# Expert loop of a hybrid decoder layer: next rows transposed before the gate/up products, the activation's transposes amid them, two result buffers, one load per weight matrix

## The reference, cut to what matters

```python
g = jnp.einsum('td,edf->tef', tb, w_eg)
u = jnp.einsum('td,edf->tef', tb, w_eu)
act = jax.nn.silu(g) * u * gb[:, :, None].astype(tb.dtype)
return jnp.einsum('tef,efd->td', act, w_ed)      # + shared expert, times the adaLN gate, plus x
```

## Time and profile before

| | us |
|---|---|
| median of 3 runs | 2066.68 (2063.21 to 2070.07) |
| the profiled execution | 2074.8 |
| its span, first to last instruction | 2072.8 |
| TensorE busy | 1651.7 (80%) |
| VectorE busy | 1330.2 (64%) |
| ScalarE busy | 926.2 (45%) |
| mean DMA rate | 174 GB/s; 335 to 352 GB/s in most of the expert stage |

### The profile page before, as it was taken

The page is one execution under the profiler, slowest core; times in us unless marked ns, Lnnn a source line. Parts: engine busy times, 40 slices in busy tenths (PEclk is TensorE's granted clock), DMA queues, the critical chain, the costliest instruction groups (busy, mean ns, idle before and its releaser), DMA issues.

```text
span 2072.8 us, 23077 instructions
## 1 busy us (share of the span) xinstructions
PE 1651.7 (80%) x7242; PEld 1276.1 (62%) x7243; DVE 1330.2 (64%) x1717; ACT 926.2 (45%) x1132; POOL 314.2 (15%) x282
## 2 busy tenths in 40 slices
PE   6697797799698798796975737899999669999860
PEld 1484685687476485584764625777777557777750
DVE  2486476546637657666446556788888337887859
ACT  2226425423233232322332225677777347777740
POOL 1000000000200202002100071123233122223210
PEclk9698998899699798897898867999999789999985
DMA  8110220244033050240520138899999449999948
GB/s 267 67 62 21 69 74 21 102 134 151 0 122 101 21 179 24 61 163 0 189 73 20 41 115 293 296 349 342 345 352 372 159 183 330 334 335 335 326 180 365
DMA packets 126064, 361.42 MB, mean 174 GB/s; under 512 B 21164, under 2 KB 31600, under 8 KB 115344
## 3 DMA queue, kind: packets, MB, share of 16 engines
q1 hardware_dynamic: 98352, 295.20, 41.0%
q0 software_dynamic: 22688, 45.29, 5.9%
q10 hardware_dynamic: 4928, 19.78, 2.4%
HBM read 352.18 MB, written 43.66 MB: 191 GB/s over the span
## 4 chain that ended last, share of the span: by engine, by line
PE 51%; DMA 24%; DVE 11%; ACT 6%; issue 5%; POOL 2%; POOLq 1%; ACTq 0%; SPq 0%; DVEq 0%
DMA y_rows<-yb,row_of 21%; PE psum L1188 13%; PE psum L1189 13%; PE psum L1190 13%; ACT yb L756 3%; PE psum L1388 2%; POOL slot_table L493 2%; PE psum L1210 1%; DVE ofin L864 1%; PE psum L1368 1%; PE psum L1342 1%; PE psum L1314 1%; DMA ysum<-y_rows 1%; PE psum L1399 1%; DMA rawm<-in_w_exp_down 1%
## 5 line engine op out<-in xcount | busy, mean ns | idle before, releaser
L784 DVE TENSOR_TENSOR ring<-rawm,ring 128x2048 fp32r<-128x2048 f32 x192 | 433.8, 2287 | 85.9 <-ACT ring L715 85.9
L715 ACT ACTIVATE ring<-rawm 128x2048 fp32r<-128x2048 f32 x192 | 355.4, 1908 | 31.1 <-DMA g_dram<-g2b 15.9
L1188 PE MATMUL psum<-ring,xT 128*128 128x512 f32 x528 | 219.5, 416 | 49.6 <-DVE xT L792 49.1
L1485 DVE TENSOR_TENSOR hl<-raw,hl 128x2048 fp32r<-128x2048 f32 x59 | 134.4, 2291 | 143.8 <-ACT hl L996 143.3
L1189 PE MATMUL psum<-ring,xT 128*128 128x512 f32 x528 | 211.9, 401 | 0.0
L1190 PE MATMUL psum<-ring,xT 128*128 128x512 f32 x528 | 211.5, 401 | 0.3 <-issue 0.3
L1188 PE MATMUL psum<-hl,hT 128*128 128x512 f32 x416 | 165.1, 397 | 11.2 <-DVE hT L1762 11.2
L996 ACT ACTIVATE hl<-raw 128x2048 fp32r<-128x2048 f32 x59 | 112.0, 1910 | 129.0 <-PE psum L1190 93.6
L1189 PE MATMUL psum<-hl,hT 128*128 128x512 f32 x416 | 162.9, 392 | 0.0
L1190 PE MATMUL psum<-hl,hT 128*128 128x512 f32 x416 | 162.8, 391 | 0.0
L1188 PEld LDWEIGHTS psum<-ring,xT 128*128 128x128 f32 x528 | 102.9, 195 | 84.3 <-DVE xT L792 41.1
(11 more groups left out here) (370 smaller groups left out, 3092.0 us busy)
## 6 DMA issues: line engine op xcount, KB each, us to landing
rawm<-in_w_exp_gate SPq DMA_DIRECT2D x128, 512.0 KB, 7.9
rawm<-in_w_exp_up SPq DMA_DIRECT2D x128, 512.0 KB, 10.7
rawm<-in_w_exp_down SPq DMA_DIRECT2D x64, 1024.0 KB, 6.8
raw<-in_w_in SPq DMA_DIRECT2D x36, 1024.0 KB, 5.2
raw<-in_w_ada SPq DMA_DIRECT2D x24, 1024.0 KB, 5.2
ysum<-y_rows ACTq DMA_DIRECT2D x16, 1024.0 KB, 9.0
raw<-in_w_branch_b SPq DMA_DIRECT2D x8, 1024.0 KB, 5.3
raw<-in_w_branch_a SPq DMA_DIRECT2D x4, 1024.0 KB, 5.1
```

Of the source, the lines that this page charges most:

```text
L715: A(ring[:, slot, 1, :], rawm[slot][:], ACT.Copy).then_inc(S["m_hi2"], 1)
L784: TT(ring[:, slot, 0, :], rawm[slot][:], ring[:, slot, 1, :].bitcast(F32), ALU.subtract).then_inc(S["m_lo2"], 1)
L1188: M(dst, lhs(0), rhs(0), start=first, stop=False)
L1485: TT(h_[:, 1, :], r, h_[:, 0, :].bitcast(F32), ALU.subtract).then_inc(S["lo_done"], 1)
```

## The change

Six edits, all in the expert stage.

- On TensorE the 8 transposes of the next rows come ahead of the 24 gate/up matmuls, and the 2 transposes of the activation of expert e-1 come after 12 of the 24. ScalarE and VectorE get the matching order: x_hi and x_lo first; ScalarE's three splits are spread over the iteration.
- yb has two buffers, each with its own semaphore (m_y0, m_y1). Place for it comes from `act`, which now lies over `upper`, a constant of the dense part.
- Each weight matrix is one load of 1 MB (8 KB in one run for each partition), three for an expert and not five; the gate/up slots wait for `xt_ps`.
- The hardware loop has 10 passes of six iterations in place of 20 of three, so that the parity of yb is known in the code.
- GpSimd issues the gather of the first extra rows one expert ahead (`first_more_rows`).
- Two pairs of semaphores of the dense part (dtT and lgT) become one pair (not shown).

```diff
@@ build: buffers
-    yb = sb("yb", [P, D])
-    act = sb("act", [P, 3, FE])
+    yb = sb("yb", [P, 2, D])
+    act = nc.alloc_sbuf_tensor_at("act", [P, 3, FE], F32, offset=upper_at)
...
-        TRIPLES = (NE - 4) // 3
+        SIXES = (NE - 4) // 6
...
@@ iterations
-            with eng.Fori(0, TRIPLES) as i:
-                for par in range(3):
-                    it(i * 3 + (3 + par), par, i + 1)
+            with eng.Fori(0, SIXES) as i:
+                for j in range(6):
+                    it(i * 6 + (3 + j), j % 3, i * 2 + (1 + j // 3), (i * 3 + (3 + j) // 2, (3 + j) % 2))
...
@@ sp_moe, load(e, par)
-                        sp.wait_ge(S["at_ps" if u < 2 else "dn_ps"], e - 2)
+                        if u < 2:
+                            sp.wait_ge(S["xt_ps"], e)
+                        else:
+                            sp.wait_ge(S["dn_ps"], e - 2)
                     buf = rawm[slot][:]
-                    if u < 2:
-                        b_ = buf.rearrange("p (s k n) -> p s k n", s=2, n=FE)
-                        for half, src in enumerate((gate, up)):
-                            sp.dma_start(b_[:, half], src[at, :, u * 4:u * 4 + 4, :].rearrange(
-                                "o p k n -> (o p) k n")).then_inc(S[f"m_raw{slot}"], 16)
-                    else:
-                        sp.dma_start(buf.rearrange("p (k n) -> p k n", n=D),
-                                     down[at].rearrange("o p k n -> (o p) k n")).then_inc(S[f"m_raw{slot}"], 16)
+                    src = (gate, up, down)[u]
+                    sp.dma_start(buf.rearrange("p (k n) -> p k n", n=FE if u < 2 else D),
+                                 src[at].rearrange("o p k n -> (o p) k n")).then_inc(S[f"m_raw{slot}"], 16)
...
-            with sp.Fori(0, TRIPLES) as i:
+            with sp.Fori(0, 2 * SIXES) as i:
...
@@ pool_moe
-                                        yb[:], None, bounds_check=T * TOPK - 1,
-                                        oob_is_err=False).then_inc(S["m_y"], 16)
+                                        yb[:, e % 2, :], None, bounds_check=T * TOPK - 1,
+                                        oob_is_err=False).then_inc(S[f"m_y{e % 2}"], 16)
...
-            def more(e):
+            def more(e, counts):
                 def body(j, x_):
                     o = lambda n: S[f"more_{n}"]
-                    more_rows(e, j, x_)
+                    if j > 1:
+                        more_rows(e, j, x_)
...
+            def first_more_rows(e):
+
+                count, n = read_counts(pool, e)
+                with pool.If(count > P):
+                    more_rows(e, 1, n)
+                return count, n
...
                 if e < NE:
-                    more(e)
+                    more(e, counts)
+                if e + 1 < NE:
+                    counts = first_more_rows(e + 1)
...
@@ pe_moe
-            def gate_up(par):
+            def gate_up(par, halfway=None):
                 for k in range(KD):
-                    wv = lambda q: ring[:, 3 * par + k // 4, 1 - q, :].rearrange(
-                        "p (s k n) -> p s k n", s=2, n=FE)[:, :, k % 4, :]
+                    if k == KD // 2 and halfway:
+                        halfway()
+                    wv = lambda q: ring[:, 3 * par:3 * par + 2, 1 - q, k * FE:(k + 1) * FE]
...
-            def it(e, par, turn):
+            def it(e, par, turn, two):
...
-                if not isinstance(e, int) or e > 0:
-
-                    pe.wait_ge(S["act_ready"], e)
-                    wait(pe, S["at_lo"], e - 1)
-                    act_to_T(act[:, prev, :]).then_inc(S["at_ps"], 1)
+
+                def act_before():
+                    if not isinstance(e, int) or e > 0:
+                        pe.wait_ge(S["act_ready"], e)
+                        wait(pe, S["at_lo"], e - 1)
+                        act_to_T(act[:, prev, :]).then_inc(S["at_ps"], 1)
+
+                if not isinstance(e, int) or e + 1 < NE:
+                    pe.wait_ge(S[f"m_x{nxt}"], turn * 16 + (32 if nxt == 0 else 16))
+                    pe.wait_ge(S["xt_lo"], e + 1)
+                    to_T(xg[:, nxt, :]).then_inc(S["xt_ps"], 1)
                 if whole:
...
-                    gate_up(par).then_inc(S["gu_ps"], 1)
-                if not isinstance(e, int) or e + 1 < NE:
-
-                    pe.wait_ge(S[f"m_x{nxt}"], turn * 16 + (32 if nxt == 0 else 16))
-                    pe.wait_ge(S["xt_lo"], e + 1)
-                    to_T(xg[:, nxt, :]).then_inc(S["xt_ps"], 1)
+                    gate_up(par, act_before).then_inc(S["gu_ps"], 1)
+                else:
+                    act_before()
...
@@ act_moe, it: the order on ScalarE
+                if more_:
+                    a.wait_ge(S["xt_ps"], e + 2)
+                    x_hi(nxt).then_inc(S["xt_hi"], 1)
+                    split(nxt, turn + (1 if nxt == 0 else 0), [0])
                 if before_:
                     a.wait_ge(S["at_ps"], e)
                     wait(a, S["dn_ps"], e - 3)
                     a_hi(prev).then_inc(S["at_hi"], 1)
                 if more_:
-                    split(nxt, turn + (1 if nxt == 0 else 0))
+                    split(nxt, turn + (1 if nxt == 0 else 0), [1])
                 if whole:
                     a.wait_ge(S["gu_ps"], e + 1)
                     wait(a, S["at_ps"], e - 2)
                     silu_to(act[:, par, :], par).then_inc(S["gu_silu"], 1)
                 if more_:
-                    a.wait_ge(S["xt_ps"], e + 2)
-                    x_hi(nxt).then_inc(S["xt_hi"], 1)
+                    split(nxt, turn + (1 if nxt == 0 else 0), [2])
                 if before_:
                     a.wait_ge(S["dn_ps"], e)
-                    if not isinstance(e, int) or e > 1:
-
-                        a.wait_ge(S["m_y"], e * 16 - 16)
-                    A(yb[:], psum[:, 5:7].rearrange("p b n -> p (b n)"), ACT.Copy).then_inc(S["y_ev"], 1)
+                    if not isinstance(e, int) or e > 2:
+
+                        a.wait_ge(S[f"m_y{1 - two[1]}"], two[0] * 16 - (0 if two[1] else 16))
+                    A(yb[:, 1 - two[1], :], psum[:, 5:7].rearrange("p b n -> p (b n)"), ACT.Copy).then_inc(S["y_ev"], 1)
...
@@ vec_moe, it: x_lo(nxt) comes first
+                if more_:
+                    v.wait_ge(S["xt_hi"], e + 2)
+                    x_lo(nxt).then_inc(S["xt_lo"], 1)
                 if not isinstance(e, int) or e > 0:
                     v.wait_ge(S["at_hi"], e)
                     a_lo(prev).then_inc(S["at_lo"], 1)
...
                 if more_:
-                    v.wait_ge(S["xt_hi"], e + 2)
-                    x_lo(nxt).then_inc(S["xt_lo"], 1)
                     split(nxt, e + 1, [2])
```

More of the change, by code:

```diff
@@ L192, in build @@
     ident = sb("ident", [P, P])
+    upper_at = sb.at
     upper = sb("upper", [P, P])
@@ L341, in build @@
             "proj_free", "hi_done", "lo_done", "mod_used", "mod_ps", "mod_ev", "par_T", "par_ev",
[L342 removed]
+            "silu_c", "xr_ready", "xT_ps", "h_tmp", "h_hi", "h_lo", "small_hi", "small_lo", "dt_ps", "smallT_ps", "smallT_ev",
             "dt_exp", "dt_dve", "dt_a", "cum_ps", "cum_exp", "trig_in", "trig_out", "sq_done")
@@ L357, in build @@
         sem(*[f"m_raw{i}" for i in range(9)])
-        sem("m_hi2", "m_lo2", "m_x0", "m_x1", "m_x2", "m_y", "xt_ps", "xt_hi", "xt_lo", "gu_ps", "gu_silu", "act_ready",
+        sem("m_hi2", "m_lo2", "m_x0", "m_x1", "m_x2", "m_y0", "m_y1", "xt_ps", "xt_hi", "xt_lo", "gu_ps", "gu_silu", "act_ready",
             "at_ps", "at_hi", "at_lo", "dn_ps", "y_ev", "held")
@@ L511, in read_counts, with extra @@
             return [eng.value_load(cnt[0:1, q, bass.ds(e, 1)], min_val=0, max_val=T) for q in range(2)]
-        def extra(eng, e, body):
-            count, n = read_counts(eng, e)
+        def extra(eng, e, body, counts=None):
+            count, n = counts or read_counts(eng, e)
             with eng.If(count > P):
@@ L524, in iterations @@
             for e in range(3):
-                it(e, e, 0)
-            with eng.Fori(0, TRIPLES) as i:
-                for par in range(3):
-                    it(i * 3 + (3 + par), par, i + 1)
+                it(e, e, 0, (e // 2, e % 2))
+            with eng.Fori(0, SIXES) as i:
+                for j in range(6):
+                    it(i * 6 + (3 + j), j % 3, i * 2 + (1 + j // 3), (i * 3 + (3 + j) // 2, (3 + j) % 2))
             for e in range(NE - 1, last):
-                it(e, e % 3, e // 3)
+                it(e, e % 3, e // 3, (e // 2, e % 2))
         def sp_moe(sp):
@@ L609, in body @@
                     hold(pool, o("s"), x_ * 16 + 16)
-                extra(pool, e, body)
+                extra(pool, e, body, counts)
+            def first_more_rows(e):
[3 more added lines that the diff above has]
+                return count, n
             for e in range(3):
                 gather(e)
+            counts = first_more_rows(0)
             for e in range(NE + 1):
@@ L709, in act_moe, with split @@
```

(30 more changed lines are left out.)

## The result

The changed kernel takes 2121.38 us (median of 4 runs, 2119.59 to 2126.51) against 2068.38 for the kernel before: a ratio of 1.026, 95% interval 1.0243 to 1.0285. It is slower by 53 us, where 2060 was forecast with a range to 2098. The profiled execution took 2126.5 us; its span, from the first to the last instruction, is 2124.8.

A forecast was written before the change was run, and what follows sets the result against it. TensorE was taken as nearest its limit, 9.56 of 10.48 us an iteration. Wins of 53 + 24 = 77 us less 69 lost took 2074.8 profiled to 2067; with the median 8.1 us lower, 2059, said as 2060; range 1990 to 2098.

The forecast's parts named there:

- the term for the loop of six: TensorE's longer loop code doesn't fit and is fetched anew each pass, with waits at jumps back and skips: 69 us lost.
- What bounds the kernel: Expert stage: TensorE is nearest its limit, busy 9.56 of 10.48 us an iteration; order alone can win the idle 0.92.
- fetched and dearer: Rival: at skips and jump back of TensorE's loop each page is waited for singly, 108 us lost, 2098 us; chance 0.19.
- The wins, 77 us: Expert stage: 53 us from the new order in 58 ordinary iterations plus 24 us from the two extra bodies.
- the rival on the transfers: Rival: DMA share 0.96 is a bound, an iteration needs 10.05 us, 49 us won with code held, 2018 us; chance 0.06.
- full, not at their limit: DMA queues in the expert stage: 333 GB/s at share 0.96 is no bound, since other stretches reached 378 and 407.
- The loads of 1 MB: Weight loads, three of 1 MB for an expert, not five: same bytes, nobody on TensorE waits for a weight, 0 us won.
- The last sign of the prediction: If TensorE waits for ring in each iteration, the claim that 8.5 and 8.1 us fit under 9.56 was wrong.
- Two yb buffers: ScalarE's 1.69 us wait for the scatter goes, letting it run at its own 8.1 us; no gain beyond the 53.
- the 53: The new order on TensorE, ScalarE and VectorE wins 0.92 us in each of 58 ordinary iterations: 53 us.
- Waits of SP: Gate/up loads wait for xt_ps and are issued at about the same place: 0 to 0.43 us an iteration, taken 0.
- Gather of xo one expert ahead: Extra bodies: TensorE's wait of 10.26 us becomes about 1.3 and the clock stays up: 12 us each, 24 for both.

The follow-up runs named there:

- pe_three: The changed kernel with TensorE and VectorE back to loops of three iterations, only ScalarE keeping six: 2017.5 us, ratio 0.975 to the kernel before.
- before_six: The kernel before with only TensorE's loop made ten passes of six iterations, order, loads and yb as before: 2182.3 us, ratio 1.053.
- p3_extra_traffic: pe_three with one more 256 KB copy within HBM for each expert, which nobody reads: 2047.2 us, ratio 0.988 to the kernel before.
- p3_xo_earlier: pe_three with the gather of the extra rows issued another iteration earlier: 2009.1 us, ratio 0.970 to the kernel before.

## Why the prediction was wrong, point by point

The step that failed is the size of the term for the loop of six: 69 us, from one jump back at 6.0 us and one waited skip at 2.1 us in a pass. The changed kernel waits at three turns in a pass, and each costs about 5.1 us. The mechanism was right.

*What bounds the kernel.* TensorE idle 0.92 us an iteration, mostly for x_lo: right, and the wait went with the order. The length of 10.48 us came from 21 scatters in 220 us; by the copies to yb an ordinary iteration takes 10.63. With the code held, the next bound stands 0.6 us below that (10.04), not 0.9 or more.

*The loop of six.* The mechanism was named and is shown: q8 forecast at 140, measured at 148; pe_three and before_six give it 104 and 113 us. The term was mis-sized. From the ninth copy to yb on, the jump back waits 2.9 to 4.0 us where no extra body comes before it, and two skips in a pass wait 2.6 to 4.6 us. In the 25 such turns without an extra body the copies to yb are 14.7 us apart, in the 27 others 9.6: 5.1 us each, of which 3.45 is the wait in the mean and most of the rest the clock (behind the 3.58 us shown, 0.94 us on the transposes and nine matmuls 0.2 us slower). So the jump was priced high if anything; the skips were one too few in each pass and priced at less than half. For the jump back I had counted the fall of the clock, from the earlier trace rows; for the skips the only rows that I had, 2.19 and 1.93 us, showed none, so I gave none. Why the skips wait longer than those is not shown by any run: perhaps the longer packets of the other queues, perhaps the fetch of a page that the engine had dropped. before_six, with the old 4 KB runs, has 125.2 us in 39 waits, which speaks against the packets.

With the measured pieces the sum closes: 28 waits over 2.5 us at 5.1 us are 143, less the 8 that the old first pass pays 135; 77 - 135 is 58 us slower, 2125, where 2121 was measured. This is an estimate, since it prices the waits of the first pass and behind the extra body like the others. The rival "fetched and dearer" had this sign; it was given 0.19 and 108 us. That this is near the 104 of pe_three is luck: it puts 8.3 us on the jump and 2.1 on each of two skips.

*The wins, 77 us.* In the changed kernel they came about as forecast: 9.6 us in the turns that don't wait for code, against 10.63, ScalarE hardly waiting for weights, and the two extra bodies short. As the rival on the transfers said, waiting for code gives the queues time, so this step is not what put the changed kernel outside the range. It fails where the code is held, and this fits with pe_three giving the loop 104 us and not 135: pe_three measures the wins alone at 2.5%, 52 us, close to the 49 of that rival, and in it ScalarE waits 76 us for up and down weights in the expert stage. The failing step there is the one in which 0.96 was read as "full, not at their limit". I compared rates of other stretches (378 and 407 GB/s) that had few small packets: 628 packets under 512 B in 40 us of 1550 to 1590 are 16 in a us, 5386 in 220 us are 24. In 1400 to 1550 no run reached more than 369 GB/s; shorter stretches did (383 in 1340 to 1400 of p3_extra_traffic), so the ceiling is not sharp. The loads of 1 MB, which I gave nothing, raised it: 16 us. The last sign of the prediction, TensorE waiting for ring, appears here (31 waits), yet not because 8.5 and 8.1 us of work don't fit under 9.56: the loads that the splits wait for are late.

*Two yb buffers*, "no gain beyond the 53": wrong for the order that it goes with, 21 us. *Waits of SP*: no sign of a cost, and no run that moves them alone.

*Gather of xo one expert ahead*, 24 us. In the changed kernel the two turns with a body took 37.9 and 34.5 us where they had taken 41.4 and 41.6, 10.5 us less and not 24, although one of them has a wait for code of 7.1 us where there had been 2.2. In pe_three undoing the edit costs 4 us, 10 in the two turns themselves. I took the landing of 4.3 us as the kernel before has it, in a queue that had run empty while TensorE waited for it. The edit itself fills that queue. In pe_three the waits stayed at 7.5 and 4.1 us and the clock stayed down in both bodies (1.97 us for the transposes), so its 5 us of the sum went with them.

*The chances.* The sum was only 8 us from a change of sign, and slower had 0.30. The range's upper end of 2098 was the price of the dearer rival; above it 0.09 was left, without a price.

## What to carry to other kernels

Before unrolling a hardware loop further, count its code, bodies behind untaken branches included, against what the engine has been seen to keep, and unroll only the engine that needs the distinction. Take a DMA share of 0.95 as the next bound until a stretch with the same mix of packets shows more bytes. A latency read where the queues were empty is not the latency that a prefetch will see.

## What was not expected of the hardware

- TensorE keeps a loop whose code is 5.9 packets of 16 KB long (47 fetches in all) and fetches one of 7.2 anew in each pass (126); of 9.5 or so, 148. The price was 104 to 113 us for ten passes, against 31 us at 7.2, where almost only the jump back is waited for.
- Behind a wait of 3.58 us TensorE ran at 1.2 GHz for the next 5 us or so; a turn of the changed kernel that waits for code costs 5.1 us in the mean for a wait of 3.45.
- With all weights in runs of 8 KB queue q1 moved 24.2 KB per us and DMA engine, with two thirds of them in runs of 4 KB 22.2, beside the same indirect transfers.
- An indirect gather landed after 4.3 us in empty queues and after 8.5 to 11.2 in full ones (pe_three, p3_xo_earlier); in the changed kernel, whose queues are at 0.80 to 0.83, after 5.3 and 8.5.
